# Turnover between the sub-layers of a fp32 diffusion trunk: sums of squares taken ahead, and h made tile by tile

## What is computed

```python
def adaln(cond, w, b):
    return (jax.nn.silu(cond) @ w + b)[:, None, :]
def rmsnorm(x, g):
    return x * lax.rsqrt(jnp.mean(x * x, axis=-1, keepdims=True) + EPS) * g
def pre_norm(x, mod, j, g):
    return rmsnorm(x, g) * (1 + mod_chunk(mod, 3 * j + 1)) + mod_chunk(mod, 3 * j)
def post_residual(x, out, mod, j, g, w):
    return x + w * mod_chunk(mod, 3 * j + 2) * rmsnorm(out, g)
```

## Time and profile before

| what | value |
|---|---|
| runs | 1885.96, 1886.35, 1888.42 us; median 1886.35 |
| the profiled execution: its own time | 1889.84 us |
| its span, first to last instruction | 1888.0 us |
| PE / PE weight load busy | 1727.4 / 1655.3 us |
| DVE / ACT / POOL busy | 809.5 / 644.6 / 150.5 us |
| mean granted clock of TensorE | 0.955 of full |
| DMA | 260.5 MB, 138 GB/s on average |

### The profile page before, as it was taken

The page is one execution under the profiler, slowest core; times in us unless marked ns, Lnnn a source line. Parts: engine busy times, 40 slices in busy tenths (PEclk is TensorE's granted clock), DMA queues, the critical chain, the costliest instruction groups (busy, mean ns, idle before and its releaser), DMA issues.

```text
span 1888.0 us, 27571 instructions
## 1 busy us (share of the span) xinstructions
PE 1727.4 (91%) x11455; PEld 1655.3 (88%) x11455; DVE 809.5 (43%) x1113; ACT 644.6 (34%) x1035; POOL 150.5 (8%) x92
## 2 busy tenths in 40 slices
PE   4899999789997899799999889999969997999996
PEld 3799999688885788699999789999959996999996
DVE  1544433343321876643433463343354556444334
ACT  1533333233332124533323343332333344333332
POOL 0100000310110350200000200000030002000001
PEclk9999999889998699899999899999989998999998
DMA  9434364644436662433353434335343354433310
GB/s 320 153 111 133 117 195 132 210 120 121 79 77 166 213 217 82 144 128 133 119 178 132 162 102 134 117 127 185 128 156 112 112 179 134 148 119 128 101 61 34
DMA packets 256234, 260.50 MB, mean 138 GB/s; under 512 B 6770, under 2 KB 254099, under 8 KB 256147
## 3 DMA queue, kind: packets, MB, share of 16 engines
q1 hardware_dynamic: 251074, 254.02, 41.4%
q0 software_dynamic: 1072, 2.62, 1.9%
q10 hardware_dynamic: 4000, 2.62, 0.5%
HBM read 256.62 MB, written 2.62 MB: 137 GB/s over the span
## 4 chain that ended last, share of the span: by engine, by line
PE 86%; DVE 6%; DMA 3%; ACT 3%; issue 1%; SPq 1%; POOL 0%; ACTq 0%; DVEq 0%
PE bank L365 22%; PE bank L366 22%; PE bank L367 22%; PE bank L379 3%; PE bank L380 2%; PE bank L381 2%; PE bank L1423 2%; PE bank L1207 2%; PE bank L1236 2%; DMA MIX<-in_b_rpb 1%; DVE RSTD L853 1%; DMA RAW<-in_mod_w 1%; DVE X L913 1%; DVE TT L909 1%; PE bank L1384 1%
## 5 line engine op out<-in xcount | busy, mean ns | idle before, releaser
L333 DVE TENSOR_TENSOR WL<-RAW,WH 128x1024 fp32r<-128x1024 f32 (+1 forms) x316 | 379.5, 1203 | 794.2 <-ACT WH L319 793.6
L319 ACT ACTIVATE WH<-RAW 128x1024 fp32r<-128x1024 f32 (+1 forms) x344 | 356.8, 1040 | 754.7 <-PE bank L367 686.5
L365 PE MATMUL bank<-HH,WH 128*128 128x384 f32 x1664 | 565.7, 340 | 9.1 <-ACT TT L619 6.0
L366 PE MATMUL bank<-HL,WH 128*128 128x384 f32 x1664 | 563.5, 339 | 0.0
L367 PE MATMUL bank<-HH,WL 128*128 128x384 f32 x1664 | 563.4, 339 | 0.0
L365 PEld LDWEIGHTS bank<-HH,WH 128*128 128x128 f32 x1664 | 312.2, 188 | 13.7 <-DVE WL L333 7.3
L366 PEld LDWEIGHTS bank<-HL,WH 128*128 128x128 f32 x1664 | 312.2, 188 | 0.0
L367 PEld LDWEIGHTS bank<-HH,WL 128*128 128x128 f32 x1664 | 312.2, 188 | 0.0
L365 PE MATMUL bank<-AH,WH 128*128 128x384 f32 x704 | 239.4, 340 | 2.1 <-ACT MOD L559 2.1
L366 PE MATMUL bank<-AL,WH 128*128 128x384 f32 x704 | 239.1, 340 | 0.0
L367 PE MATMUL bank<-AH,WL 128*128 128x384 f32 x704 | 239.0, 339 | 0.0
(11 more groups left out here) (159 smaller groups left out, 1456.2 us busy)
## 6 DMA issues: line engine op xcount, KB each, us to landing
RAW<-in_ffn_w_in SPq DMA_DIRECT2D x88, 1024.0 KB, 5.1
RAW<-in_mod_w SPq DMA_DIRECT2D x72, 1024.0 KB, 5.3
RAW<-in_ffn_w_out SPq DMA_DIRECT2D x32, 1024.0 KB, 5.4
RAW<-in_ab_w_in SPq DMA_DIRECT2D x16, 1024.0 KB, 8.3
RAW<-in_ffn_w_out SPq DMA_DIRECT2D x16, 768.0 KB, 5.0
RAW<-in_cv_w_in SPq DMA_DIRECT2D x12, 1024.0 KB, 5.1
RAW<-in_ab_w_out SPq DMA_DIRECT2D x4, 1024.0 KB, 7.3
RAW<-in_cv_w_out SPq DMA_DIRECT2D x4, 1024.0 KB, 5.3
```

What stands on the lines that cost most here:

```text
L319: e.activation(WH[:, (2 * m + b) % 4, 0:nk, :], RAW[:, p, 0:nk, b * P:(b + 1) * P], ACT.Copy).then_inc(half_hi, 1)
L333: e.tensor_tensor(WL[:, k, 0:nk, :], RAW[:, p, 0:nk, b * P:(b + 1) * P], WH[:, k, 0:nk, :].bitcast(F32), ALU.subtract).then_inc(half_ready, 1)
L365: e.matmul(out, WH[:, k, kk, :], xh(kk), start=(first and kk == 0), stop=False)
L366: e.matmul(out, WH[:, k, kk, :], xl(kk), start=False, stop=False)
```

## The change

Five things are done at once; the diff is cut to what they need.

1. **Sums ahead.** With y = OUT (scaled by the gate) and r the token's rstd, the new sum of squares of X + r·y is ΣX² + r·(2·ΣXy + r·Σy²). While the output tiles come, ACT also makes y² and DVE adds it to `RSTD`, multiplies X by OUT and adds it to `ROOT` (for each tile one more ACT pair and three more DVE instructions). After the last tile PE sums `ACC`, `RSTD`, `ROOT` and the last tile's three products over the partitions with matmuls of one moving column.
2. **Token-wise chain.** Root, reciprocal and the algebra run on 128x3 (token on the partition, three token tiles); PE spreads a result back over the partitions with three matmuls against the identity (`spread`) into PSUM banks 4 and 5.
3. **X and h tile by tile.** DVE and ACT go through the eight tiles once, as below; ACT makes high part and whole h from the third tile on. `first_four` starts with the high part alone, and keeps its last two tiles back to finish bank by bank.
4. **One modulation group inside the turnover**, five eighths of its first pair before the second spread; modK and modL move into the first FFN's output stage, the former middle group of the third sub-layer becomes its between group; these output stages are written out instead of looped. The between group's turn stands after the first pair of the next sub-layer. The order of the ring is a hand-written list.
5. **Opening.** Identity, parameters and x are issued on ACT's queue, the weights at once on SP's, the masks on POOL's; ACT takes the sum of squares of x in its token layout with an accumulating Square; in0's first two slots are loaded before mod0's last two.

```diff
-MIDDLE = ("modA", "modC", "modE", "modG", "modI")
-BETWEEN = ("modB", "modD", "modF", "modH", "modJ")
-MOD_GROUPS = {"mod0": 2, "modA": 1, "modB": 2, "modC": 6, "modD": 1, "modE": 1, "modF": 1, "modG": 1, "modH": 1,
+BETWEEN = ("modB", "modD", "modE", "modH", "modJ")
+MOD_GROUPS = {"mod0": 2, "modA": 1, "modK": 1, "modL": 1, "modB": 1, "modC": 6, "modD": 1, "modE": 1, "modG": 1,
...
+    order = run("mod0", 0, 6) + run("in0", 0, 2) + run("mod0", 6, 8) + run("in0", 2, 22)
+    order += run("modA", 0, 4) + run("out0", 0, 5) + run("modK", 0, 4) + run("out0", 5, 9) + run("modL", 0, 4)
+    order += run("out0", 9, 12)
+    for s in range(1, 6):
+        order += run(f"in{s}", 0, 2) + run(BETWEEN[s - 1], 0, 4) + run(f"in{s}", 2, IN_SLOTS[kind])
...
 @block.gpsimd
-            first_splits("in0")
-            scale_out(0, OUTF)
-            first_splits("in1")
+            first_splits("in0")
+            pool.dma_start(LMASK[:], level_masks).then_inc(masks_landed, 16)
...
+            for s in range(2, 6):
+                half_low(f"in{s}")
 @block.scalar
+            def high_parts(s, first_full):
+                act.wait_ge(coef_ready, 3 * s + 2)
+                for d in range(KD):
+                    act.wait_ge(h_scaled, 8 * s + d + 1)
...
+                    a.then_inc(h_hi, 1)
+                    if d >= first_full:
+                        act.wait_ge(h_ready, 8 * s + d - 1)
...
+                        a.then_inc(h_full, 1)
+                if SUBLAYERS[s][0] == "ffn":
+                    act.activation(STAT[:, 7, 0:1], EPSC[:], ACT.Silu)
+            def turnover(s, OUT, n):
+                nxt = ahead(act, split_act, s, "out", n)
+                out_tile(s, OUT, st, n, 0, 6)
+                nxt[0]()
+                tile_squares(s, st, n, 1, 7)
+                nxt[1]()
+                root(bank[0][:, 0:3], 0, (stat_done, 2 * s + 1))
+                tile_scaled(s, OUT, 7)
+                root(STAT[:, 4, :], 5, (sum_step, 5 * (s + 1)))
+                high_parts(s + 1, 2)
+                mod_rows_out(between(s + 1))
...
             def ffn(s):
...
+                for n in range(11):
+                    for half in ahead(act, split_act, s, "out", n):
+                        half()
+                    if n == 0:
+                        act.activation(STAT[:, 7, 1:2], EPSC[:], ACT.Sqrt)
+                    if n - 1 in rows_at:
+                        mod_cols_out(rows_at[n - 1])
 @block.vector
+            def turnover(s, OUT, n):
+                add_terms(s, 6, OUT)
+                split_dve(dve, f"in{s + 1}", 1, 8)[0]()
+                dve.wait_ge(out_sq, 8 * s + 8)
+                dve.tensor_tensor(TT[:, 1, :], X[:, 7, :], cols3(bank[7]), ALU.mult).then_inc(xy_done, 1)
+                one_over(0, 2 * s + 2)
...
+                scale_y(s, OUT, 0)
+                one_over(5, 2 * s + 3)
+                add_y(OUT, 0, 8 * s + 1)
+                s += 1
+                dve.wait_ge(row_bcast, 2 * s + 1)
+                scaled(s, 0)
+                full(s, 0)
+                for d in range(1, KD):
+                    scale_y(s - 1, OUT, d)
+                    low(s, d - 1)
+                    add_y(OUT, d, 8 * (s - 1) + d + 1)
+                    scaled(s, d)
+                    if d == 1:
+                        full(s, d)
+                low(s, KD - 1)
 @block.tensor
+            def turnover(s):
+                sums(sum_o, ACC, opens=True)
+                sums(sum_y2, RSTD, opens=True)
+                sums(sum_xy, ROOT)
+                pe.wait_ge(out_sq, 8 * s + 8)
+                sums(sum_o, SQ[:, 1, :], closes=True).then_inc(stat_done, 1)
+                sums(sum_xy, TT[:, 1, :], CC[:, s, 7, :])
+                sums(sum_y2, SQ[:, 1, :], CC7SQ, closes=True).then_inc(stat_done, 1)
+                pe.wait_ge(rstd_done, 2 * s + 2)
+                spread(bank[4], 1)
+                mod_pair(st, 0, range(5))
+                pe.wait_ge(rstd_done, 2 * s + 3)
+                spread(bank[5], 6)
+                mod_pair(st, 0, range(5, KD))
+                mod_pair(st, 2)
```

More of the change, by code:

```diff
@@ L107, in constants, with ring_order, run @@
     return np.eye(P, dtype=np.float32), masks, window[order], flip
-def plan():
[L112 to L134, removed]
+def ring_order():
+    def run(st, a, b):
+        return [(st, n) for n in range(a, b)]
+    order = run("mod0", 0, 6) + run("in0", 0, 2) + run("mod0", 6, 8) + run("in0", 2, 22)
+    order += run("modA", 0, 4) + run("out0", 0, 5) + run("modK", 0, 4) + run("out0", 5, 9) + run("modL", 0, 4)
+    order += run("out0", 9, 12)
+    for s in range(1, 6):
+        kind, middle = SUBLAYERS[s][0], {1: ("modC", 24), 3: ("modG", 4), 4: ("modI", 4)}
+        order += run(f"in{s}", 0, 2) + run(BETWEEN[s - 1], 0, 4) + run(f"in{s}", 2, IN_SLOTS[kind])
+        order += run(middle[s][0], 0, middle[s][1]) if s in middle else []
+        order += run(f"out{s}", 0, OUT_SLOTS[kind])
+    return order
+def plan():
+    stages, freed, place, split, mod = {}, [], {}, 0, 0
+    for st, n in ring_order():
+        if st not in stages:
+            stages[st] = dict(m=split, q=mod)
+        place[st, n] = len(freed)
+        if st.startswith("mod"):
+            mod += 1
+            freed.append(("mod", mod))
+        else:
+            split += 1
+            freed.append(("split", split))
+    for st in stages:
+        stages[st]["n"] = sum(1 for at in place if at[0] == st)
+    return stages, freed, place
 def trunk(nc, x_prompt, x_sample, c, state_hgrn, cache_k, cache_v, c_ctx, mod_w, mod_b, norm_pre, norm_post,
@@ L278, in ring_at @@
         def ring_at(st, j):
[L280 removed]
+            return place[st, j] % RING, place[st, j] // RING
         def src_of(st, n):
@@ L958, in even @@
                     proj(tau)
+                    if tau == 3:
+                        coefficients(between(s))
                 for step in range(24 + 3):
@@ L1203, in mod_pair @@
                 at = (q // 2) * P
-                for kk in range(KD):
+                for kk in steps:
                     for strip in range(4):
@@ new lines, in sums, with spread @@
+            def sums(out, src, weight=None, opens=False, closes=False):
+                for t in range(TOKS):
+                    w = ONES[:, 0:1] if weight is None else weight[:, min(t, 1):min(t, 1) + 1]
+                    mm = pe.matmul(out[:, t:t + 1], src[:, t * P:(t + 1) * P], w,
+                                   start=opens and t == 0, stop=closes and t == TOKS - 1)
+                return mm
+            def spread(B, at):
+                for t in range(TOKS):
+                    mm = pe.matmul(B[:, t * P:(t + 1) * P], STAT[:, at, t:t + 1].broadcast_to([P, P]), IDENT[:],
+                                   start=True, stop=True)
+                mm.then_inc(row_bcast, 1)
```

591 lines of the change are left out of this document (328 added, 263 removed).

## The result

The changed kernel takes 1821.78 us (median; 1821.32 to 1822.13) against 1886.15 for the kernel before on the same chip: ratio 0.9658, 95% interval 0.9646 to 0.9671, so 64.4 us less. Its profiled execution took 1821.55 us, its span is 1819.7 us, its mean granted clock 0.961 (0.955 before).

What follows compares the result with a forecast made beforehand. PE, busy in 1727 of 1888 us, was taken to bound the kernel. Terms -42 - 13.5 - 4 + 9 = -50.5 took 1889.84 to 1839.3 us, 1836 for the median; range 1812 to 1860.

Steps and rivals of the forecast that it cites:

- rivals A to D: Chance, us: A low clock 0.14, 1858; B opening nil 0.10, 1849; C ring fails 0.04, 1776; D dear ring 0.05, 1906.
- turnovers: Five stretches between sub-layers, from last output matmul through the first four columns: 247.8 becomes 205.9 us, minus 42.
- opening: Kernel start: first matmul at 45.3 instead of 57.73, stream resuming at 64.8 instead of 78.50; minus 13.5 us.
- end: After the last sub-layer: 17 us instead of 21.2, as half the transposes come early; minus 4.
- the rest of the stream: Modulation work and waits moved into PE's matmul stream: 30.3 us against 21.6 today, plus 9, bounds plus 4 and plus 14.
- the waits behind the column copy: Output stages: PE waits for ACT's column copy, 0.7 us at modK and modL, 2.2 at modA and modG.
- The ring: h tiles in a turnover: ACT's instructions, then DVE's low, add_y and scaled in a circle, 3.7 us a tile.
- The tail: End of a turnover: the last 24 matmuls wait for tile 7, then run partly at half clock, 6.2 us.
- the start: From a turnover's last output matmul through sums, spreads and small steps: low(0) ends at 9.5 us, first matmul at 9.7.
- PE's 5/8 of a pair ... ends at 6.1, so it hides: Modulation matmuls before a turnover's second spread: 5/8 of half of 3.70 us, over at 6.1, costing nothing.
- the two spreads: In a turnover, PE spreads results over the partitions: the first takes 0.75 us, till 4.95; the second ends at 6.95.
- POOL beside DVE: Turnovers: POOL's split ends before DVE's steps, so no slowdown counted; bounds 0 and 1.5 us a turnover.

Runs made afterwards that it cites:

- a_noshift: The changed kernel with STAT and CC7SQ put behind the mixers' buffer, so HH, HL, AH and AL are back at their earlier addresses: 1849.22 us.
- b_shift: The kernel before with an unused tensor of 128 bytes per partition ahead of EPSC, so HH, HL, AH, AL lie 128 bytes higher: 1861.26 us.
- a_ring: The changed kernel with DVE's add and scaled product of a tile put ahead of the low part of the tile before: 1782.36 us.
- r_mod2: a_ring plus a shorter tail, later Sqrt preload and second mod pair behind tile 0; then 16 modulation matmuls, not 40, ahead of the second spread: 1764.86 us.
- r_mod8: a_ring with all 8 mod0 slots loaded ahead of the first in0 slot: 1786.72 us.

## Why the prediction was right, and where it wasn't

The forecast was 1836 us, the result 1821.8, inside its range, and none of the rivals A to D came: the clock of the turnovers is 0.84 to 0.88, the opening gives its share, rounds take neither 2.1 nor 5.7 us. But two errors of opposite sign met, and that is luck. The written change was forecast at 50.5 us and gave 36 to 40; the addresses, of which the prediction says nothing, gave 24 to 27. Without them the median is 1849.22 (a_noshift), still in the range, but 13 us above the forecast where the result is 14 below it.

Profiled execution against profiled execution, 68.3 us less (1889.84 to 1821.55), by the prediction's terms:

| term | forecast | measured | from | against b_shift |
|---|---|---|---|---|
| turnovers | -42 | -32.0 | 247.8 to 215.8 | -28.0 |
| opening | -13.5 | -14.3 | 78.50 to 64.23 | -11.3 |
| end | -4 | -4.0 | 21.19 to 17.15 | -4.1 |
| the rest of the stream | +9 | -18 | the remainder | +6.0 |

The last column sets the changed kernel's trace beside that of b_shift (1858.83 us), which has the same pitch; its five turnovers last 243.8 us. By it the turnovers are 14 us short of the forecast, not 10: the profiled execution of before lies 3.5 us over its median.

**The stream.** The term +9 counted added work only, and took the matmuls of the rest as they were. 7296 of the 7872 matmuls lie outside the first four columns of a sub-layer, and 3.4 ns each is 24.8 us; without that the term is +6.8. Stage by stage against b_shift, which has the same pitch, the moved work comes to +6.0: +12.8 in the first FFN's output stage, -5.9 in the third sub-layer, -0.9 in the others together. So the waits behind the column copy were sized rightly (forecast 2.2, measured 2.17 at modA) and the term was some 2 to 3 us too dear. What failed is a step the prediction didn't have: that an added tensor moves others, and with them the pitch. No row of before could price it, but that the diff allocates ahead of HH could be read.

**The turnovers, 10 to 14 us short.** The ring was read rightly, with 3.54 us a round for the forecast 3.7, and a_ring shows that its order alone makes it: turned round, it is 2.11. The tail was right too, 6.15 us (377.42 to 383.57) for 6.2. Wrong was the start, which was priced at full clock. In the prediction's count of time the second spread was to start at 6.2 and the first matmul at 9.7; in the first turnover it is 8.5 and 12.6. The step "PE's 5/8 of a pair ... ends at 6.1, so it hides" was made from 3.70 us for 128 matmuls at full clock; at half clock the 40 took 2.3 us for 1.2 (346.98 to 349.27), in the way of the second spread. And the two spreads, counted at 0.75 each, took 1.6 each (345.42 to 346.98 and 349.27 to 350.85). So of the 2.9 us 1.1 are the modulation matmuls, 1.6 the spreads and 0.4 the sums; the matmuls behind them took 0.2 less. In the third and fourth, whose clock falls later, the first matmul is at 11.0; behind the two mixers (second and fifth) at 14.2 and 14.4, since there PE first waits 1.2 to 1.4 us for DVE's sum over the output tiles, which the prediction had as hidden. The 43.30, 44.35 and 45.09 us stretches are these. r_mod2 gets back 5.6 us by the order of the modulation matmuls alone.

**The opening.** Last pair at 39.12 (forecast 39), first matmul at 45.94 (45.3), stream at 64.23 (64.8). Against b_shift, whose first stage ends at 242.03 where the changed kernel's ends at 230.72, it is 11.3 us; the forecast lies between the two readings. r_mod8 bears out that bytes set the pair's time, and shows what the sum didn't say: the first tile hangs as much on ACT's order, and on POOL being done, as on the pair.

**POOL beside DVE.** Counted at nothing, and rightly in the turnovers: in the first one POOL's split lies at 342.58 to 344.92, ahead of the first of DVE's five steps at 345.66, and no DVE instruction in the five turnovers is stretched. r_mod8 is where it strikes.

**Slips in the working.** L853 takes 2.55 us in the earlier trace rows, not 3.27; the number enters no sum. DMA moves 319 GB/s at 10 to 15 us and reaches 348 to 350 only from 15 us on. 34.7 and 6.2 are 40.9, not 41.1, and 45.3 and 19.3 are 64.6, not 64.8. The four bounds of 12, 5, 2 and 5 us add up to 24, so the range holds them all at once.

## What to carry to other kernels

When a wait is turned into a ring of short steps, write down the circle: the order of two instructions on one engine (low part ahead of the next product, or behind it) was worth 39 us here, as much as the whole change it was part of. Work put on PE beside a chain hides only if it is over, at the clock that is granted there (0.51 here, though PE was never idle), before what the chain needs next. And a kernel that is three quarters one matmul form (7872 at 176.7 ns are 1391 of 1888 us) should be compared with a copy whose only difference is where its operands lie, before a gain is put down to the change.

## What was not expected of the hardware

The start-to-start pitch of the 128x384 fp32r matmuls depends on where the buffers with their moving operands start in SBUF: 173.3 ns at 96 modulo 256, 176.7 at 224, at a granted clock of 1.00, with the same instructions, the same stationary operands and the same neighbours; values between, of 174.0 to 176.0, at other placements. It is 2% of a pitch, and 24 to 27 us of this kernel. Nobody should take a rule from this: at 160 modulo 256 one stage has 174.3 and the others 176.7.
The Trainium skill ("SBUF — State Buffer", section "Operand start alignment") lets an fp32 operand start at any multiple of 4 bytes and says that the rule is "about legality, not speed"; all placements here are multiples of 4, and their times differ.
The Trainium skill ("TensorE: Matmul & The Clock Gate", section "Back-to-back issue gap") gives N/2.4 + 2.5 ns for an isolated matmul; for N = 384 that is, as an estimate from the page, 162.5 ns. The matmuls here aren't isolated: each comes in a stream with a weight load of its own, and no placement tried came under 173.3.
